# Sixteen projection blocks moved from the stick-breaking stage into the opening stage, and one convolution tap onto ScalarE

## The reference

```
u = rms_norm(x) * gain                    # 1024 tokens x 1024
proj = u @ w_in                           # to q, k, v, z, xbc, dt, mem_q, gate logits
y_sb  = stick_breaking_attention(q, k, v)             # 16 heads of 64
xbc   = silu(causal_depthwise_conv(xbc_raw, w, b))    # 4 taps, 3072 channels
y_ssd = ssd(xbc, dt) * silu(z), grouped RMSNorm
y_mem = softmax(mem_q @ k_mem) @ v_mem
merged = sum of sigmoid(gates_i) * (y_i @ w_i);  mix = merged @ w_o;  then a squared-ReLU MLP
```

## Time and profile before

| | before |
|---|---|
| median of 3 runs | 2694.46 us (2691.84 to 2698.86) |
| the profiled execution, its own time | 2688.13 us |
| its span, first to last instruction | 2686.4 us |
| mean granted TensorE clock | 0.990 |
| busy over the span: PE, DVE, ACT, POOL | 97%, 69%, 44%, 49% |
| opening stage | 0 to 336 us |
| stick-breaking stage | 336 to 1098 us |

### The profile page before, as it was taken

How to read it: one execution, slowest core, us unless ns; L and a number is a source line. 1 busy time by engine, 2 the same in 40 slices (tenths; PEclk the granted TensorE clock), 3 DMA queues, 4 the chain that set the end, 5 groups by cost and what they waited for, 6 DMA issues and landing times. The chain is left out here.

```text
span 2686.4 us, 35512 instructions
## 1 busy us (share of the span) xinstructions
PE 2597.0 (97%) x12752; PEld 2175.4 (81%) x12752; DVE 1850.0 (69%) x2063; ACT 1191.2 (44%) x2098; POOL 1313.1 (49%) x809
## 2 busy tenths in 40 slices
PE   7999999999999999799999899999998999999998
PEld 6888888888888888688888777878887788888886
DVE  5666476777677677498888656653258887768567
ACT  5533144444444444467666544443144222244443
POOL 3233255454554554288888743545600676535224
PEclk9999999999999999899999999999999999999999
DMA  4634443433324341467666653434331444376574
GB/s 160 204 151 160 153 149 105 126 102 109 112 94 134 110 119 62 137 175 210 196 207 202 226 189 133 152 134 149 126 126 55 150 160 166 129 245 211 203 253 146
DMA packets 208108, 411.53 MB, mean 153 GB/s; under 512 B 19648, under 2 KB 100160, under 8 KB 207936
## 3 DMA queue, kind: packets, MB, share of 16 engines
q1 hardware_dynamic: 207936, 409.27, 46.0%
HBM read 289.01 MB, written 120.19 MB: 152 GB/s over the span
## 5 line engine op out<-in xcount | busy, mean ns | idle before, releaser
L1451 POOL TENSOR_TENSOR sb_beta<-sb_beta,sb_rest 128x128 f32<-128x128 f32 (+7 forms) x128 | 164.1, 1282 | 371.4 <-DVE sb_rest L1509 371.4
L1279 PE MATMUL sb_psg<-uh,sb_wl 128*128 128x512 f32 x768 | 309.7, 403 | 0.0
L1279 PE MATMUL sb_psg<-ul,sb_wh 128*128 128x512 f32 x768 | 304.3, 396 | 0.0
L1279 PE MATMUL sb_psg<-uh,sb_wh 128*128 128x512 f32 x768 | 302.8, 394 | 0.0
L3169 PE MATMUL ff_ps<-ff_mh,ff_total 128*128 128x512 f32 x896 | 278.6, 391 | 4.6 <-DVE ff_total L3672 4.6
L1509 DVE TENSOR_TENSOR_SCAN sb_rest<-sb_rest 128x128 f32<-128x128 f32 (+7 forms) x128 | 187.3, 1463 | 115.1 <-ACT sb_rest L1395 114.8
L3169 PEld LDWEIGHTS ff_ps<-ff_mh,ff_total 128*128 128x128 f32 x896 | 169.4, 189 | 41.0 <-issue 5.7
L2314 PE MATMUL first_ps<-uh,mg_wh 128*128 128x512 f32 x480 | 193.3, 403 | 6.2 <-DVE ul L2519 4.9
L2314 PE MATMUL first_ps<-ul,mg_wh 128*128 128x512 f32 x480 | 188.5, 393 | 0.0
L2314 PE MATMUL first_ps<-uh,mg_wl 128*128 128x512 f32 x480 | 188.3, 392 | 0.0
L3169 PE MATMUL ff_ps<-ff_ml,ff_total 128*128 128x512 f32 x448 | 175.2, 391 | 0.0
(11 more groups left out here) (422 smaller groups left out, 7259.6 us busy)
## 6 DMA issues: line engine op xcount, KB each, us to landing
sb_w<-in_w_in SPq DMA_DIRECT2D x48, 512.0 KB, 4.4
scratch_proj<-sb_out SPq DMA_DIRECT2D x48, 512.0 KB, 2.9
ff_w<-in_w_down SPq DMA_DIRECT2D x96, 256.0 KB, 3.4
sb_k<-scratch_qk SPq DMA_DIRECT2D x64, 256.0 KB, 6.1
ssd_arow<-scratch_decay SPq DMA_DIRECT2D x32, 512.0 KB, 5.6
mg_gate<-scratch_proj SPq DMA_DIRECT2D x32, 512.0 KB, 3.6
ff_w<-in_w_up SPq DMA_DIRECT2D x32, 512.0 KB, 3.7
mg_w<-in_w_branch SPq DMA_DIRECT2D x30, 512.0 KB, 4.5
```

The costliest lines, as they stand in the source:

```text
L1279: last = nc.tensor.matmul(ps_g[:, h], l[:, s, k], r[:, k, h * HALF:(h + 1) * HALF], start=(k == 0 and j == 0), stop=(k == KB - 1 and j == 2))
L1451: nc.gpsimd.tensor_tensor(beta[:, i % 3, 0:cols], beta[:, i % 3, 0:cols], rest[:, i % 3, 0:cols], ALU.mult).then_inc(weighted, 1)
```

## The change

Eight of the sixteen gate blocks (Z_EARLY) and all eight memory queries become pairs of the opening stage, 19 pairs instead of 11. A gate pair gets its sigmoid on ScalarE (`sigm_of_tile`) and its product on VectorE (`gate_of_tile`) at the start of the next pair's turn, and its store waits for the product. 32 blocks are left in the stick-breaking stage, in the order "xxxz", with 6 fewer matmuls in every step. Tap 0 of the convolution goes to ScalarE as one instruction with a scale and a bias (`first_tap`), `padded` is doubled, and the output tile of a block is m % 2 for all kinds. In the opening stage the order of VectorE is changed in the loop over the tiles, the splits of the quarter sums go to items 2, 5, 8 and 11 of the memory loop, and the split of the first pair's weights goes from item 15 to items 13 and 14.

```diff
+Z_EARLY = 8
-    BLOCK_PAIRS = [(b, b + 1) for b in range(2, Z0, 2)]
+    BLOCK_PAIRS = [(b, b + 1) for b in (*range(2, Z0 + Z_EARLY, 2), *range(MQ0, G0, 2))]
+    FIRST_GATED, N_GATED = (Z0 - 2) // 2, Z_EARLY // 2
+    T_ITEMS = (2, 5, 8, 11)
...
+                    if is_gate(c):
+                        sp.wait_ge(gated, gates_to(c, row))
                     sp.wait_ge(c22_made if row else c11_made, c + 1)
                     sp.wait_ge(c21_made if row else c12_made, c + 1)
                     sp.dma_start(proj[b], tiles[:, x]).then_inc(out_stored[x], 16)
...
+        def sigm_of_tile(c, row):
+            act.wait_ge(c22_made if row else c11_made, c + 1)
+            act.wait_ge(c21_made if row else c12_made, c + 1)
+            act.wait_ge(hi_stored[row], 16 * N_SPLIT)
+            if c > FIRST_GATED:
+                act.wait_ge(gated, gates_to(c - 1, row))
+            nc.scalar.activation(sigm[:, row], tiles[:, 2 * (c % 2) + row], ACT.Sigmoid).then_inc(tile_sigm, 1)
...
         for m in range(N_KV):
-            if 1 <= m <= 4:
-                round_t(m)
+            if m in T_ITEMS:
+                round_t(T_ITEMS.index(m) + 1)
...
-            if m == 15:
+            if m == 13:
                 round_front(0)
+            if m == 14:
+                for which in (S1, S2, S3):
+                    round_back(which, 0)
...
-        for which in (S1, S2, S3, A22, S4):
+        for which in (A22, S4):
             round_back(which, 0)
...
+            if c and is_gate(c - 1):
+                for row in range(2):
+                    sigm_of_tile(c - 1, row)
...
+        def gate_of_tile(c, row):
+            dve.wait_ge(tile_sigm, gates_to(c, row))
+            x = tiles[:, 2 * (c % 2) + row]
+            nc.vector.tensor_tensor(x, x, sigm[:, row], ALU.mult).then_inc(gated, 1)
...
-        for i in range(TILES + 2):
-            if i >= 3:
-                rest_of_u(i - 2)
-            if i < TILES:
-                invert(i)
-            if 0 < i <= TILES:
-                scale_turned(i - 1)
-            if i == 2:
+        for i in range(2):
+            invert(i)
+        scale_turned(0)
+        for i in range(1, TILES):
+            if i == 1:
                 rest_of_u(0)
-            if i == TB - 2:
+                scale_turned(1)
+                rest_of_u(1)
+                invert(2)
+            else:
+                scale_turned(i)
+                if i + 1 < TILES:
+                    invert(i + 1)
+                rest_of_u(i)
+            if i == TB - 3:
                 take_decays(0)
...
-    kinds = "xzxzxq"
+    kinds = "xxxz"
-    AT_STEP = (11, 13, 15, 17, 19, 21, 23, 25)
+    AT_STEP = (5, 7, 9, 11, 13, 15, 17, 19)
...
+        def first_tap(m):
+            n, s = convs_before(m), m % 2
+            act.wait_ge(drained[0], n + 1)
+            act.wait_ge(drained[1], n + 1)
+            if n == 0:
+                act.wait_ge(small_loaded, 32)
+            if m >= 2:
+                act.wait_ge(g_stored[s], (m // 2) * 16)
+            nc.scalar.activation(out_tile[:, s], padded[:, n % 2, 0:S], ACT.Identity, scale=cw[:, n, 0:1],
+                                 bias=cb[:, n:n + 1]).then_inc(tapped, 1)
...
+                if kind_of(m) == "x" and ends(m, 1) == i:
+                    first_tap(m)
...
                 if kind_of(m) == "x" and i == end + 1:
-                    convolve(m, range(2))
+                    convolve(m, range(1, 2))
                 if kind_of(m) == "x" and i == end + 2:
                     convolve(m, range(2, CONV))
```

More of the change, by code:

```diff
@@ L1021, in vector @@
                     lo_of_tile(c - 1, row)
+            if c and is_gate(c - 1):
+                for row in range(2):
+                    gate_of_tile(c - 1, row)
             if more:
@@ L1402, in scalar @@
                 hi(u)
-            for m in range(0, FILL, 2):
-                if i == ends(m, 1) + 3:
+            for m in range(FILL):
+                if kind_of(m) == "x" and i == ends(m, 1) + 3:
                     sigmoid_of_conv(m)
```

90 lines of the change are left out of this document (46 added, 44 removed).

## The result

The changed kernel takes 2728.9 us (median of 4 runs, 2724.8 to 2731.6) against 2693.8 us (2691.8 to 2698.9) before: ratio 1.0126, interval 1.0107 to 1.0145. It is slower by 1.3%, outside the range of 2663 to 2718 us, and on the other side of the forecast of 2690. The profiled run took 2731.6 us with a span of 2729.8, as much above its span as before.

The account below looks back on a forecast made before the run. TensorE was taken as the bound, with SBUF access shared by GpSimd and VectorE near it after the change. Moved blocks -21.8, opening edits -5, new waits +22 gave -5 us: 2690 us, range 2663 to 2718.

Parts of the forecast that it names:

- The quarter products: Opening stage: 8 more pairs of 84 matmuls add 152.5 us; gate and query extras cost nothing, bound 0 to 5 us.
- TensorE's own time in the stage: Stick-breaking stage: with 16 blocks gone TensorE needs 753 - 174 = 579 us.
- The walk: One group of eight steps in the stick-breaking stage, followed instruction by instruction: about 1.4 us of waits a group, 22 us.
- the second wait: TensorE before weighing values, on VectorE's low halves: 0.3 us a group, 1.2 where the second block is a conv block.
- the first wait: TensorE before transposing step 7's weights, on VectorE's first low half of step 6: 0.9 us a group.
- The clock: Rival: waits lower TensorE's clock, up to 1.7 us each time, +10 to +25 us on some groups; chance 0.08.
- The opening edits: Opening stage: VectorE's new tile order and earlier first weight split gain 5 us; bounds 8 gained and 3 lost.
- The shared access decides: Rival: SBUF access shared by GpSimd and VectorE delays the low halves; 56 us of waits, +29, 2724 us; chance 0.20.
- the third rival: Waits lower the clock in the stick-breaking stage, or opening pairs run late: 2705 to 2718 us; chance 0.08.

Follow-up runs that it names:

- h2: Kernel before with only the memory queries moved: h1 plus block matmuls redistributed over the steps and the gate half delayed only for blocks ending at t = 7; 2687.6 us, ratio 0.9980.
- e3: Changed kernel with the second half of the gate product one step later, behind the next head's first scan; 2723.0 us.
- e1: Changed kernel with the opening's old VectorE order in the loop over the tiles put back; 2727.1 us.
- d4: c2 with the first head's own matmul split and, for blocks ending at t = 7, the SiLU product one step later; 2690.6 us.
- d2: c2 with one weight rounding a step earlier and a matmul split of its own for the first head; 2692.6 us.
- b1: Kernel before, nothing moved, with the first tap on ScalarE and the first pair's weights split two items earlier; 2711.6 us.
- e2: Changed kernel with the rounding of the blocks' weights moved from GpSimd to ScalarE; 2720.0 us.
- f2: Changed kernel with taps 2 and 3 of each conv block left out (not computed); 2689.9 us.
- e4: Changed kernel with block matmuls redistributed towards a head's first two and last two steps; 2707.7 us.
- h1: Kernel before with only the memory queries moved, old tile order, weight rounding on ScalarE, one tap a step, gate half a step later; 2715.0 us.
- d3: d2 with the SiLU of a block ending at t = 7, its sigmoid too, one step earlier; 2732.3 us.
- c2: c1 with a milder split of the block matmuls over the steps; 2695.8 us.
- b2: b1 with the first tap one step later in ScalarE's order; 2688.4 us, ratio 0.9980.
- c1: Changed kernel with the edits of e1, e2, e3 and e4 together, and the taps spread one a step; 2708.4 us.

## Why the prediction was wrong

- **The quarter products** (+152.5 us, no cost for gates and queries): right, +151.5 us. Sigmoids, products and stores of the gate pairs stayed hidden.
- **TensorE's own time in the stage** (579 us): right as far as a run shows it; h2 is within 7 us of the same working with 8 blocks more. So the move is worth 22 us if nothing else waits.
- **The walk** is the step that failed: 22 us of waits, 58 us found above TensorE's own time, of which 40 are waits and 15 the clock. Places and engine were right (t = 1 and t = 2, low halves of VectorE), and so was the second wait (7.2 us where 8 were forecast). The term that was mis-sized is the first wait, the one for the transposes: 0.9 us a group, 14 us in all, and measured 31.4. In the eight groups without a gate half it was about right (1.1 us on average). In the eight with one it was 2.8, for two reasons that the gate group shows: I had GpSimd's rounding put scan 6 off by 0.3 us, and it made it 1.0 us longer; and I put the gate half behind the low half that the transposes wait for, where it stands in front (e3: 0.5 us a group). I walked one group and took its wait for all sixteen.
- **The clock.** I held half clock to be a rival of its own with a chance of 0.08. It was 15 us of the 58, in seven places and the start (in e1, with the same stage, 7 us in three places and the start). It should have been a term of the sum wherever a wait of about 2 us was possible, since the earlier trace rows had shown such a case. The runs that shorten the waits also lose it: d4 has no window below full clock.
- **The start of the stage**, costed at nothing: a wait of 5.65 us, where the kernel before has one of 1.87. ScalarE's first rounding of transposed weights waits for the opening's last stores, 8.9 us where it was 3.3 before, and the short first steps no longer hide it. d2 got 5 us back by giving the first head its own split.
- **The opening edits** (5 gained): 1.7 lost. By the means of e1's comparison the tile order lost about 3 us, and the earlier weight split gained 1 to 3 (125.0 and b1's 122.8 against the single 126.2 of before). I had counted the waits that would go and only one that would come.
- **The rest of the kernel** was 6.4 us longer in the profiled run. Not all of it is the same code: the first 27.0 us (22.8 before), up to the next stage's first matmul, still hold the last group of this stage, and 1.9 of these 4.2 us are its two waits. Behind them comes code that is the same in all 19 kernels, and in their profiles it took 1574 to 1585 us, so a difference of some us there says nothing about an edit. What varies in it was not found.
- **The rivals.** "The shared access decides" gave +29 and 2724 us and had 0.20; that size and side came true, its first wait too (2.3 us forecast, 2.0 found), its second not (1.2, against 0.45); what made up the size instead was the clock, which belonged to the third rival, and the wait at the start. Its own reasoning holds in part: e2 shows the sharing (6 us of waits, up to 14 with the clock), and f2 that the two late taps are most of it (36 us). But it took the load as given. I had put that load at 595 us, above TensorE's 579; in the trace GpSimd or one of VectorE's scans, taps or SiLU products runs in 565 of the stage's 635 us, stretching included. That the order of the work matters with the load unchanged is shown by e4 (21 us of the kernel), by h1 against h2 (24 us of the stage) and, the other way, by d3 (37 us). How much of the 58 us is order is not shown: c2 (29 us above) and d4 (21) have the same work on VectorE, but also 30 roundings, 57 us, taken off GpSimd, and the order of c2 with the roundings left on GpSimd was not run.

What stays open: how much of the last 21 us in d4 is VectorE's sum; how order and shared access divide the gain of c2 and d4; and whether any move of blocks gains over b2, which moves none and is as fast as h2 and d4.

## What to carry to other kernels

When filler work is taken out of the engine that is the bound, its total stops being the question. Look at the slack in the tightest steps, redo the split of the filler over the steps, and put nothing long in front of the instruction that the bound waits for next; only then judge the move. An edit that adds a wait to an in-order engine costs what stands behind the wait: b1 and d3 both lost 20 to 37 us by one kind of instruction placed one step too early.

## What the runs showed of the hardware that I had not expected

- A wait of TensorE of 2.36 us in a stage otherwise full was followed by a stretch at half clock (0.77, 0.50 and 0.87 in three windows of 2 us); in the changed kernel this came seven times after the start, behind waits of 1.52 to 2.93 us, while two waits of 2.72 us were not followed by it. In e1 the same waits were followed by it three times, and one of 2.89 us was not. The groups of c1, c2, d2 and d4, with waits of up to 1.46, 1.11, 1.31 and 1.12 us behind the first group's start, had none. A wait of some 2 us is a risk here, not a fixed price.
- Taking 30 rounding instructions of 1.90 us off GpSimd shortened VectorE's taps by 0.22 us and its scans of 896 columns by 0.50 us on average. An instruction of VectorE can so be paid for by one of GpSimd that nobody waits for.
- ScalarE's first tap takes 1.24 us in all 24 instances (1241 to 1249 ns); VectorE's took 0.81 to 2.5 us for the same work. The engine that is slower alone can be the steadier place.
